# The third query chunk by input tiles, with the final norm's sums and the spread roots between them, and the fifth chunk's split behind the evictions

## What is computed

```
def first_block(...):
    ...
        x = x + g_f[:, None, :] * conv_ffn(h, w_up[l], conv_w[l], conv_b[l], w_down[l])
    return rmsnorm(x, norm_final_g)

def second_block(x, ...):
    h = x
    for i in range(DEPTH_2):
        hn = rmsnorm_2(h, attn_norm[i])
        if i % N_MIXERS == 0:
            ...
            m = diff_attention(hn, w_in[i], w_out[i], diff_lambda[li], diff_subln[li], lambda_init_fn(i))
        else:
            m = moba_attention(hn, w_in[i], w_out[i])
        h = h + m
        h = h + squared_relu_mlp(rmsnorm_2(h, mlp_norm[i]), w_ff1[i], w_ff2[i])
    return rmsnorm_2(h, final_norm)

def diff_attention(h, w_in, w_out, lam_params, subln_w, lam_init):
    ...
    q, k, v = jnp.split(h @ w_in, 3, axis=-1)
    ...
```

## Time and profile before

| | |
|---|---|
| median of three runs | 995.05 us |
| the profiled execution's own time | 995.04 us |
| its span, first to last instruction | 993.0 us |
| TensorE busy | 984.6 us, 99% of the span |
| VectorE busy | 719.3 us, 72% |
| ScalarE busy | 599.5 us, 60% |
| TensorE's granted clock, mean | 0.999 of full speed |

### The profile page before, as it was taken

How to read it: one execution, slowest core, us unless ns; L and a number is a source line. 1 busy time by engine, 2 the same in 40 slices (tenths; PEclk the granted TensorE clock), 3 DMA queues, 4 the chain that set the end, 5 groups by cost and what they waited for, 6 DMA issues and landing times.

```text
span 993.0 us, 16615 instructions
## 1 busy us (share of the span) xinstructions
PE 984.6 (99%) x6618; PEld 886.3 (89%) x6618; DVE 719.3 (72%) x1226; ACT 599.5 (60%) x1019; POOL 0.4 (0%) x5
## 2 busy tenths in 40 slices
PE   9999999999999999999999999999999999999997
PEld 8899999998888888999999888888999899888886
DVE  5898988878888888977668656565766457565562
ACT  4779665557565656867747455545665446555452
POOL 0000000000000000000000000000000000000000
PEclk9999999999999999999999999999999999999999
DMA  9965777535656564653335655555543337555521
GB/s 368 404 232 195 275 253 256 213 128 212 212 191 237 216 246 170 215 210 128 128 126 215 211 197 185 175 208 202 216 177 128 128 107 259 205 173 183 201 83 42
DMA packets 28443, 196.32 MB, mean 198 GB/s; under 512 B 3152, under 2 KB 3664, under 8 KB 5584
## 3 DMA queue, kind: packets, MB, share of 16 engines
q1 hardware_dynamic: 28224, 195.01, 55.5%
q10 hardware_dynamic: 144, 0.26, 0.1%
HBM read 194.21 MB, written 1.05 MB: 197 GB/s over the span
## 4 chain that ended last, share of the span: by engine, by line
PE 77%; DVE 14%; ACT 6%; issue 2%; POOLq 0%; DVEq 0%; ACTq 0%
PE PS L1420 16%; PE PS L1307 10%; PE PS L1105 8%; PE PS L1106 7%; PE PS L1107 7%; DVE wlo L1994 7%; PE PS L1311 5%; PE PS L1258 3%; PE PS L1261 3%; PE PS L1259 3%; ACT whi L1583 2%; ACT PB L1879 2%; PE PS L1341 2%; DVE PB L2474 2%; PE PS L1342 2%
## 5 line engine op out<-in xcount | busy, mean ns | idle before, releaser
L1994 DVE TENSOR_TENSOR wlo<-raw,whi 128x1024 fp32r<-128x1024 f32 (+1 forms) x306 | 357.7, 1214 | 60.5 <-ACT whi L1583 57.8
L1583 ACT ACTIVATE whi<-raw 128x1024 fp32r<-128x1024 f32 x300 | 297.9, 1047 | 58.5 <-PE PS L1420 52.9
L1307 PE MATMUL PS<-HX,whi 128*128 128x512 f32 x736 | 230.9, 395 | 0.0
L1311 PEld LDWEIGHTS PS<-HX,wlo 128*128 128x128 f32 x736 | 138.3, 188 | 32.3
L1105 PE MATMUL PS<-HX,whi 128*128 128x256 f32 x496 | 145.0, 292 | 0.6 <-DVE HX L1969 0.6
L1311 PE MATMUL PS<-HX,wlo 128*128 128x256 f32 x736 | 144.6, 278 | 0.0
L1106 PE MATMUL PS<-HX,whi 128*128 128x256 f32 x496 | 140.2, 283 | 0.0
L1107 PE MATMUL PS<-HX,wlo 128*128 128x256 f32 x496 | 140.1, 282 | 0.0
L1307 PEld LDWEIGHTS PS<-HX,whi 128*128 128x128 f32 x736 | 114.5, 189 | 2.6
L1105 PEld LDWEIGHTS PS<-HX,whi 128*128 128x128 f32 x496 | 94.8, 191 | 6.0 <-issue 4.3
L1106 PEld LDWEIGHTS PS<-HX,whi 128*128 128x128 f32 x496 | 94.9, 191 | 0.2
(11 more groups left out here) (287 smaller groups left out, 1808.5 us busy)
## 6 DMA issues: line engine op xcount, KB each, us to landing
raw<-wall SPq DMA_DIRECT2D x151, 1024.0 KB, 5.0
raw<-wada SPq DMA_DIRECT2D x18, 1024.0 KB, 5.0
raw<-wall SPq DMA_DIRECT2D x8, 512.0 KB, 16.4
GA<-wada SPq DMA_DIRECT2D x2, 1024.0 KB, 21.2
GA<-alibi SPq DMA_DIRECT2D x1, 2048.0 KB, 9.2
X<-xt SPq DMA_DIRECT2D x1, 1024.0 KB, 5.0
KM<-wada SPq DMA_DIRECT2D x1, 1024.0 KB, 14.2
QF<-wada SPq DMA_DIRECT2D x1, 1024.0 KB, 16.9
```

What stands on the lines that cost most here:

```text
L1307: e.matmul(PS[:, b + nt, :], whi[place(n)][:, at + nt * 128:at + nt * 128 + 128], HX[:, k, :, :].rearrange("p h t -> p (h t)"), start=k == ...
L1311: m = e.matmul(PS[:, b + nt, 0:T], wlo[place(n)][:, at + nt * 128:at + nt * 128 + 128], Hh[:, k, :], start=False, stop=k == 7, skip_group_ ...
L1583: e.activation(whi[place(n)][:, c], raw[i % RAW][:, c], ACT.Copy).then_inc(*up("a_whi", (n, half)))
L1994: e.tensor_tensor(wlo[place(n)][:, c], raw[i % RAW][:, c], f32(whi[place(n)][:, c]), ALU.subtract).then_inc(*up("v_wlo", (n, half)))
```

## The change

In the second block's first layer only:

- the third chunk is multiplied by input tiles: eight `part` steps in place of two `rows`;
- the sums of `SQ` still stand in front of it; the sums of `sum2`, which had stood right behind them, and with them the roots' steps on ScalarE and VectorE, are a step of their own (`total_both`) in front of the input tile 2; on TensorE they so come 12 matmuls later;
- the spread of the roots and its copy stand in front of input tile 6 instead of between the two output tiles: 36 matmuls of the chunk in front of it instead of 24;
- the split of the fifth chunk, which had its place in front of the third chunk, is no longer asked for there, so the next `refill`, behind the three evictions, puts it into the list together with the sixth chunk's.

```diff
--- before.py
+++ after.py
@@ -633,7 +633,8 @@
                     emit("root_table")
             elif k == 8:
                 total(a, 3)
-                refill(NUMBER[(f"qkv{layer}", 0)])
+                if layer == 1:
+                    refill(NUMBER[("qkv1", 0)])
 
         def norm_rows():
             emit("spread", a, 3)
@@ -654,7 +655,22 @@
                     emit("ev_qk", n, b, layer, "Q", 1)
                     refill(waiting[1][0])
 
-                rows(key, a, between=norm_rows, evac=ev_three)
+                if layer == 0:
+                    n = NUMBER[key]
+                    ensure(n)
+                    b = bank()
+                    for k in range(8):
+                        if k == 2:
+                            emit("total_both", a, 3)
+                        elif k == 6:
+                            norm_rows()
+                        emit("part", n, a, b, k)
+                    st["done"] = n
+                    ev_three(n, b, 0)
+                    after()
+                    refill(n)
+                else:
+                    rows(key, a, between=norm_rows, evac=ev_three)
             elif c < 4:
                 rows(key, a, evac=lambda n, b, pr, c=c: emit("ev_qk", n, b, layer, "Q", c))
             elif c < 8:
@@ -1168,9 +1184,9 @@
                 elif name in FOLDED:
                     on.wait_ge("v_sq", (name, "folded"))
                     sums(b, 0, [SQ[:, 2, :]], name)
-                    if name == "a0":
-                        on.wait_ge("v_sq", ("final", "folded"))
-                        sums(b, 2, [sum2[:, 0:T]], "both")
+            elif step == "total_both":
+                on.wait_ge("v_sq", ("final", "folded"))
+                sums(a[1], 2, [sum2[:, 0:T]], "both")
             elif step == "spread":
                 name, b = a
                 on.wait_ge("d_small", 0)
@@ -1632,7 +1648,7 @@
                 e.activation(SQ[:, nt, :], X[:, 6 + nt, :], ACT.Square).then_inc(*up("a_sq", (name, 3, nt)))
             elif step == "ev_out_tile":
                 x_at[6 + a[2]] = ("v_x", ("out", 6 + a[2]))
-            elif step == "total" or step == "total_tile" and a[2] == 1:
+            elif step == "total" and a[0] != "a0" or step == "total_both" or step == "total_tile" and a[2] == 1:
                 name, b = a[0:2]
                 if name == "a0":
                     on.wait_ge("t_sq", "both")
```

## The result

The changed kernel took 998.12 us (median of eight runs, 995.98 to 998.34), the kernel before 995.27 us beside it (eight runs, 994.82 to 995.77). The ratio is 1.0026, with an interval of 1.0015 to 1.0037. The forecast was 996.0, with a range to 996.7: too low, and 2.85 us above the kernel before is more than the 2.0 us that the prediction took for no change. One of the eight runs, 995.98, lies where the forecast is. It had a mean granted clock of 0.999, the other seven 0.997.

The account below looks back on a forecast made before the run. TensorE, busy 984.6 of 993.0 us, was taken as the bound, with time only where it waits. The 0.84 us gained is lost at the first turn and 1.02 more: 995.04 + 1.02, rounded to 996.0; range 995.7 to 996.5, wider 994.8 to 996.7.

Parts of the forecast that it names:

- The gain at the sums: Third chunk on TensorE: no wait at PB's sums, 0.80 us gained, fourth chunk starting 0.84 us earlier.
- 23 starts: Third chunk's matmuls from 414.92 to 417.75: first step 0.20 us, others 0.12, used to price a run of matmuls.
- three restarts: Third chunk on TensorE: 0.08 us each after another kind of work; without them the forecast change is about +0.75.
- The split behind the evictions: VectorE: six halves behind the evictions put the first head's scores at 428.49, 1.43 us later; ScalarE's table load delays nothing.
- The first turn: TensorE waits over 1 us for VectorE's scaling; second head's scores start at 432.69 instead of 431.67, 1.02 us later.
- Afterwards: From the third head's scores, VectorE's 0.55 us wait shrinks by 0.41; all that follows is moved by 1.02 us.
- the sum 995.04 + 1.02: Whole kernel: profiled time before plus the loss after the first turn, rounded to 996.0 us.
- The gain stays: Rival: no wait at the first turn, TensorE keeps its 0.84 us, 994.2 us; chance 0.12.
- a draw: Rival: VectorE makes up about 1 us of its 1.43, the turn costs what the sums gave, 995.0; chance 0.10.
- more is lost: Rival: the whole 1.43 us reaches TensorE, 996.5, or 997.1 if a second turn pays 0.6; chance 0.08.

Follow-up runs that it names:

- e3: The changed kernel with five matmuls on ones, never read, in TensorE's list ahead of the first turn: 996.06 us, ratio 1.0012.
- a3_after: The changed kernel itself, unaltered, run again later beside other runs: 995.95 us, ratio 1.0016; its profiled execution took 995.88 us.
- e2: The kernel before with only the fifth chunk's split moved behind the evictions: 997.04 us, ratio 1.0019.
- e8: The changed kernel with the fifth and sixth chunks' splits both ahead of the roots: 1000.02 us, ratio 1.0050.
- e5: The changed kernel with first-layer splits one chunk later for six chunks, the twelfth chunk's split where VectorE and ScalarE have time: 993.93 us, ratio 0.9990.

## Why the prediction was wrong

**The gain at the sums: right.** Sums of `PB` at 414.97 in the run that starts like the one before (forecast near 415.1), spread at 418.29 (418.6), fourth chunk at 420.37 (420.6), each with no wait but the bank's. TensorE gained 1.09 us here (420.37 against 421.46), with 0.05 of that from the start; I had 0.84. Each pair of sums took 0.37 us (415.52 to 415.89 in the first profile after), where I had 0.47 from a pair that had waited; that is the 0.2 us. (Where the prediction counts 23 starts, they are the 23 steps between 24 starts, and without its three restarts the sum is +0.78, not +0.75; neither changes the forecast.)

**The split behind the evictions: right.** VectorE's scores come at 428.24 in that run (forecast 428.49, 427.06 before), and the table load on ScalarE held up nothing.

**The first turn: right.** I said a wait of over 1 us and scores at 432.69; it is 1.38, and the scores stand at 432.44 there: 0.77 us behind the 431.67 of the earlier trace rows, 0.82 when the start is taken off, for a forecast of 1.02.

**Afterwards: right without the fall.** The loss stayed: the run's span is 993.8 for 993.0. VectorE's wait for the third head's scores shrank only from 0.55 to 0.40, not by the 0.41 of the forecast, because its wait for ScalarE at the split ahead had given back 0.24 already (0.69 before, 0.45 now). The 15 runs without a fall have a median of 995.9, and e3, which takes the fall away and leaves VectorE as late, 996.0, that is, 0.6 to 1.0 us above the kernel before beside them. That is the predicted time. VectorE in `a3_after`:

```profile
428.24 0.28 DVE L2325 CUSTOM_DVE_ANT_0 PB<-PS,GA 128x128 f32<-128x128 f32 x1
...
441.20 0.29 DVE L2325 CUSTOM_DVE_ANT_0 PB<-PS,GA 128x128 f32<-128x128 f32 x1 [0.40 <-PE PS L1524]
```

**The step that failed** is the first turn's price, "It waits. How it goes on after such a wait is shown by the fourth head", and with it the sum 995.04 + 1.02. I priced the wait by its length, with the clock at 1.00 on both sides as the earlier trace rows have it, and the head that I took for its end, the fourth, has a wait of only 0.17 at its turn (below). The sum had no term for what TensorE does after a wait of 1.4 us with little work behind it: in half of the executions its clock falls to 1.2 GHz for some 3 us, 1.55 us more. Seven of the first eight runs had it, so that the median is 2.85 us above the kernel before (998.12 - 995.27), past my bound of 2.0 us. The prediction looked for time only where TensorE waits, from its busy share of 99%; but TensorE at 1.2 GHz counts as busy too: the 2.2 us more of busy time after the change, for the same records, hold the fall and the slower start. The fourth head's turn in the kernel before:

```profile
454.95 0.74 PE L1519 MATMUL PS<-SM,PB 128*128 128x128 f32 x3 [0.17 <-DVE PB L2331]
```

**The rivals.** None of them held, and none had the clock in it. "The gain stays" ended at the first turn, as argued; a draw needed VectorE to make up 1 us of its lag, and up to that turn it made up none; "more is lost" had the right sign, but by a second turn that paid, and none does so.

**What stays open** is which executions fall. In the two profiles of the changed kernel with the fall the opening matmuls took 9.15 and 9.07 us, in the one without it 8.45; but in e2's run with it 8.05. The moment at which TensorE first gets fast differs from execution to execution, and so perhaps does the moment at which it can fall, set against the same wait. The Trainium skill (TensorE: Matmul & The Clock Gate, Part 1: The HAM clock gate) says that the chip's watching is not in step with the program, so that the same kernel begins with more slow matmuls in one run than in another. The opening rows agree with that, 8.05 to 9.15 us in these four; that it also decides the falls at 433 us was not shown. Nor does the fall set in at one place behind the wait: TensorE was slow from the spread on in e8, from the second head's scores on in the changed kernel, and a few matmuls behind them in e2. Nor was it tried how little work behind the turn would be enough.

## What to carry to other kernels

Work that is moved off one hand-over on an engine that is nearly full can land on the next one, as here: look there for the wait, and give the work that has slack (here a split whose matmuls come several us later) a place behind the hand-over, as e5 did. And do not price a new wait of TensorE by its length alone: waits of 1.2 to 1.9 us ahead of short matmuls brought the clock down here in a part of the executions, for a further 1.5 us each time that a trace shows it, so such a wait wants a second case with the clock down and a chance of its own. Matmuls that nobody reads, put into the wait, took that case away (0 of 22).

## What the hardware showed that I had not expected

- The same program came in two kinds, 15 of 30 executions each. Its three traces all have the wait of 1.37 or 1.38 us; behind it TensorE ran on at 2.4 GHz in one and at 1.2 GHz in two, at a price of 1.55 and 1.54 us.
- The waits side by side: 1.68 us ahead of the spread, between full matmuls, 0 falls in 11; 1.21 us ahead of the turn, 1 in 11; 1.94 there, 2 in 6; 3.94 ahead of the spread, 4 in 4 (one by its trace, three by their times). Work in the wait: 0 in 22. Work right behind it: 0 in 11.
- The start of the program differs by up to 1.1 us between the executions named above (28 matmuls in 8.05 to 9.15 us), and of the 0.76 us between the profiles before and after 0.50 still stand at 413 us. A comparison of two single traces to a few tenths of a us has to take that off first.
